# Attention stage of a two-layer trunk: own PSUM banks for the stick scores, head 0's scores inside the last projection slot, and the first output slot begun pair by pair

## Chip, cores and metric

One core of one Trainium2 chip. The metric is device time in microseconds, from start to end of one execution. The kernel is one program; nothing else runs on the core.

## What is computed

A trunk of two layers over 512 frames of width 1024. Layer 0 mixes by pooling and a state space; layer 1, where the change lies, mixes by two attentions, each of 8 heads of width 64. Every layer ends in a squared-ReLU MLP of width 4096. Cut to what the change touches:

```python
def _cd_mixer(h, w_in, w_out):
    qc, kc, vc, qi, ki, wi, qd, kd, vd = jnp.split(h @ w_in, offs, axis=-1)
    oc = _dsa_mixer(...)            # indexer picks 128 keys a query; softmax with ALiBi over them
    od = _stick_breaking_mixer(...) # z = q k^T / 8; log_keep = log_sigmoid(-z);
                                    # w = exp(log_sigmoid(z) + later sum of log_keep); w @ v
    return jnp.concatenate([oc, od], axis=-1) @ w_out
```

## The kernel before

**Engines and tiles.** Time lies in 4 blocks of 128 (NB = 4). Each of the engines has its own instruction stream, ordered by hand, with semaphores between them. TensorE (PE) has 8 PSUM banks of 512 float32. A weight slot is 1024 x 256: SyncE loads it, ScalarE (ACT) writes the rounded part `w_hi` (L707), VectorE (DVE) the rest `w_lo` (L1157), and PE makes 2 tiles of it, each of 8 products over k with 3 matmuls each (`product`): 48 matmuls a slot. Projection tiles go round banks 0 to 3. Slots of the values (`vd`, `vc`) are cut into 4 tiles, one for each block b.

**Projection of layer 1.** Slots in the order qi, ki, qd, kd, vd, qc, kc, vc, two slots each save ki. ACT copies every tile out (`copy_tile`, L765). From slot qd0 (`index_first`) on, PE also makes the indexer's scores, 8 a slot for three slots, ACT does their ReLU and DVE adds them to `score`. DVE then takes the 128 largest of blocks 1 to 3 in 48 rounds (MAX8 L1400 and MATCH_REPLACE8 L1402), 6 rounds a slot from the fourth of these slots on, and after the last slot writes `dsel` (`selected_distances`), the distances of the chosen keys.

**Attention steps.** Step s begins softmax head s and stick head s^1 and carries on those of the steps before. PE in step s: `scores(s,0)`, `scores(s,1)`, `outputs(s-2)`, `scores(s,2)`, `scores(s,3)`, `prob_transposes(s-1)`, `stick_sums(s-1)`. `scores(s,n)` is a pair of 64-row matmuls, which run beside each other: softmax scores into bank 4 + n%2, stick scores into bank n%2. Transposes go to bank 4 + n%2, the sums of the stick head (products of `sp_sb` with `tri` and `ones`) to bank 2 + j%2, outputs to banks 7 and 6. Because transposes share banks with the softmax scores, `prob_transposes(s-1)` waits until DVE has read rows n = 2 and 3 of step s (`s_used`).

DVE in step s: for n = 0 to 3 score plus ALiBi (L1454) and negated maximum (L1458), with `softplus_sum(s-1)` (L1441, 128 x 1280) after n = 1; then |z| into `sp_sb` (L1464); in steps 3, 5, 7 `out_lo` (L1436); then z minus the sums (L1473), four times; then four times a reciprocal (L1478) and a scaling (L1480). ACT in step s: z out of PSUM (L899), transposes out of PSUM (`pT`, L907), in steps 3, 5, 7 `out_hi` (L886), exponentials of the softmax (L916) and of the stick head (L923), then Exp and Ln of |z| (L926, L928). GpSimd (POOL) zeroes the non-causal part of four diagonal blocks (`keep_causal`, L650), of `sp_sb` after L1441 and of z after L923; PE's sums wait for the first, `outputs` for the second. Step 8 has no new scores, and step 9 only `outputs(7)`. After it ACT and DVE make the last pair of `h_hi` and `h_lo` tiles, and the four output slots (`plain_slots`) follow, then norm and MLP, in which PE is busy throughout.

## Time and profile before

| what | value |
|---|---|
| median of 3 runs | 1387.94 us (1386.94 to 1389.24) |
| the profiled execution | 1387.05 us, of which 1385.3 us span |
| PE, DVE, ACT, POOL busy | 91%, 59%, 32%, 12% of the span |
| last projection tile to first output matmul | 845.2 to 966.03 us |

The profiled execution is 0.9 us under the median. A timeline row gives the start in us from the start of the span, the duration, the engine, the line, the operation and its operands; "x4" merges neighbours of one kind, and brackets give the idle time of the engine before it and who ended it. PEclk is the share of full clock that TensorE was granted. Step s begins here where DVE starts L1454 of that step: step 6 at 923.7 and step 7 at 937.1 us.

### The profile page before, as it was taken

What the parts mean: (1) busy time and instruction counts of PE and PEld (TensorE: products, weight loads), DVE (VectorE), ACT (ScalarE), POOL (GpSimd) and SP (SyncE); (2) the same over time, 40 slices, a digit from 0 to 9 for tenths busy, and PEclk for the clock granted to TensorE, in tenths of its full rate; (3) what the DMA queues carried; (4) which work ended last, traced back from release to release, by engine and by line L of the source; (5) the groups of instructions that cost most, each with busy time, mean ns of one, the idle gap of its engine ahead of it and who ended that gap; (6) DMA issues with size and microseconds to landing.
All of it is one profiled execution on the core that took longest, in us unless ns stands there. A gap on an engine that the chain in (4) does not pass through costs nothing.

```text
span 1385.3 us, 16190 instructions
## 1 busy us (share of the span) xinstructions
PE 1265.3 (91%) x6140; PEld 1025.2 (74%) x6140; DVE 812.4 (59%) x1132; ACT 438.4 (32%) x589; POOL 159.8 (12%) x172
## 2 busy tenths in 40 slices
PE   4548858899999999999999997888999999999999
PEld 4347756688888888888877986555878888888887
DVE  2989887666555465556436797875363344343432
ACT  1223213133132141232334225775233132231321
POOL 1700540310000000006000000111400000000022
PEclk9769958999999999999999999999999999999999
DMA  8235745735444544453122331000323322323311
GB/s 261 68 99 148 195 128 187 238 114 188 162 157 164 168 159 165 151 185 91 61 92 62 97 110 37 1 1 1 91 84 99 91 91 91 91 91 105 103 64 61
DMA packets 136912, 157.68 MB, mean 114 GB/s; under 512 B 24168, under 2 KB 117536, under 8 KB 136864
## 3 DMA queue, kind: packets, MB, share of 16 engines
q1 hardware_dynamic: 121808, 151.72, 33.7%
q10 hardware_dynamic: 14480, 3.74, 1.5%
q0 software_dynamic: 576, 1.57, 0.4%
q8 instruction: 30, 0.49, 0.1%
q14 instruction: 18, 0.15, 0.0%
HBM read 151.65 MB, written 4.19 MB: 112 GB/s over the span
## 4 chain that ended last, share of the span: by engine, by line
PE 75%; DVE 16%; DMA 3%; ACT 2%; ACTq 2%; issue 1%; POOL 0%; DVEq 0%; SPq 0%
PE psum L1510 73%; DMA ada_ring<-in_ada_w 3%; DVE w_lo L1157 2%; DVE ada_acc L990 1%; PE psum L1514 1%; DVE work L1174 1%; ACTq L693 1%; DVE bz L961 1%; DVE h_lo L1186 1%; DVE sp_sb L1441 1%; DVE work L961 1%; ACT w_hi L707 1%; DVE s_t L961 1%; DVE work L1454 0%; DMA u_scratch<-ub 0%
## 5 line engine op out<-in xcount | busy, mean ns | idle before, releaser
L1510 PE MATMUL psum<-h_hi,w_hi 128*128 128x512 f32 x880 | 346.3, 394 | 18.0 <-DVE w_lo L1157 9.0
L1510 PE MATMUL psum<-h_lo,w_hi 128*128 128x512 f32 x880 | 343.8, 391 | 0.0
L1510 PE MATMUL psum<-h_hi,w_lo 128*128 128x512 f32 x880 | 343.5, 390 | 0.0
L707 ACT ACTIVATE w_hi<-w_raw 128x2048 fp32r<-128x2048 f32 x92 | 174.8, 1900 | 353.2 <-PE psum L1510 316.0
L1157 DVE TENSOR_TENSOR w_lo<-w_raw,w_hi 128x2048 fp32r<-128x2048 f32 x92 | 213.8, 2324 | 107.1 <-ACT w_hi L707 106.8
L1510 PEld LDWEIGHTS psum<-h_hi,w_hi 128*128 128x128 f32 x880 | 165.1, 188 | 58.7 <-issue 13.1
L1510 PE MATMUL psum<-a_hi,w_hi 128*128 128x512 f32 x512 | 202.4, 395 | 0.0
L1510 PE MATMUL psum<-a_hi,w_lo 128*128 128x512 f32 x512 | 202.2, 395 | 0.0
L1510 PE MATMUL psum<-a_lo,w_hi 128*128 128x512 f32 x512 | 202.1, 395 | 0.0
L1510 PEld LDWEIGHTS psum<-h_hi,w_lo 128*128 128x128 f32 x880 | 165.1, 188 | 35.7
L1510 PEld LDWEIGHTS psum<-h_lo,w_hi 128*128 128x128 f32 x880 | 165.3, 188 | 34.7
L1305 DVE SCALAR_TENSOR_TENSOR xT<-psum,mods,xT 128x512 f32<-128x512 f32 x80 | 59.2, 749 | 192.8 <-PE psum L1510 192.7
L1350 DVE TENSOR_TENSOR work<-work 128x512 f32<-128x512 f32 x64 | 44.2, 690 | 127.4 <-ACT work L840 126.6
L1510 PEld LDWEIGHTS psum<-a_hi,w_lo 128*128 128x128 f32 x512 | 96.3, 188 | 22.9
L1510 PEld LDWEIGHTS psum<-a_lo,w_hi 128*128 128x128 f32 x512 | 96.3, 188 | 22.8
L1510 PEld LDWEIGHTS psum<-a_hi,w_hi 128*128 128x128 f32 x512 | 96.3, 188 | 22.7
L840 ACT ACTIVATE work<-psum 128x512 f32<-128x512 f32 x64 | 38.2, 598 | 212.3 <-PE psum L1510 212.3
L562 POOL TENSOR_TENSOR sumsq<-xT 128x512 f32<-128x512 f32 x4 | 4.2, 1042 | 724.4 <-DVE xT L1305 724.4
L1340 DVE SCALAR_TENSOR_TENSOR ada_acc<-ada_l_ring,pb,ada_acc 128x768 f32<-128x768 f32 x56 | 60.0, 1071 | 1.1
L1354 DVE TENSOR_TENSOR a_lo<-work,a_hi 128x512 fp32r<-128x512 f32 x64 | 44.3, 692 | 2.6
L990 DVE SCALAR_TENSOR_TENSOR ada_acc<-ada_ring,pb,ada_acc 128x768 f32<-128x768 f32 x28 | 32.2, 1150 | 20.0 <-DMA ada_ring<-in_ada_w 18.5
L566 POOL TENSOR_TENSOR sumsq<-sumsq,work 128x512 f32<-128x512 f32 x24 | 43.7, 1819 | 1.9
(279 smaller groups left out, 1487.6 us busy)
## 6 DMA issues: line engine op xcount, KB each, us to landing
w_raw<-in_mlp_w SPq DMA_DIRECT2D x64, 1024.0 KB, 5.4
ada_l_ring<-in_ada_w SPq DMA_DIRECT2D x64, 384.0 KB, 6.1
ada_ring<-in_ada_w SPq DMA_DIRECT2D x40, 384.0 KB, 4.4
w_raw<-in_cd_w_in SPq DMA_DIRECT2D x14, 1024.0 KB, 5.1
ada_first<-in_ada_w SPq DMA_DIRECT2D x24, 384.0 KB, 3.9
w_raw<-in_ab_w_in SPq DMA_DIRECT2D x4, 1024.0 KB, 6.5
w_raw<-in_ab_w_out SPq DMA_DIRECT2D x4, 1024.0 KB, 8.2
w_raw<-in_cd_w_out SPq DMA_DIRECT2D x4, 1024.0 KB, 5.1
```

The source lines that it names most:

```text
L566: ins = pool.tensor_tensor(sumsq[:, :], sumsq[:, :], work[3][:, 0:L], ALU.add)
L693: act.dma_start(bb[ri][:, :, :], src[0].rearrange("(t g) p c -> (g p) t c", g=2)).then_inc(b_in, 16)
L707: act.activation(w_hi[n % 2][:, :, 0:w], raw[n % 2][:, :, 0:w], ACT.Copy).then_inc(hi_ready, 1)
L840: act.activation(work[t % 2][:, 0:L], bank[(t0 + t) % 4], ACT.Relu)\
L961: own(dve.tensor_tensor(o, a, b, op))
L990: ins = dve.scalar_tensor_tensor(out=acc[:, :], in0=buf[:, at_, :], scalar=pb[:, k:k + 1], in1=acc[:, :], op0=ALU.mult, op1=ALU.add)
L1157: dve.tensor_tensor(w_lo[n % 2][:, :, 0:w], raw[n % 2][:, :, 0:w], w_hi[n % 2][:, :, 0:w].bitcast(F32), SB).then_inc(lo_ready, 1)
L1305: dve.scalar_tensor_tensor(out=xT[:, k, :], in0=bank[t % 4], scalar=mods[:, a, 16 + k:17 + k], in1=xT[:, k, :], op0=M, op1=A).then_inc(dve ...
L1340: ins = dve.scalar_tensor_tensor(out=ada_acc[:, :], in0=src, scalar=pb[:, k:k + 1], in1=ada_acc[:, :], op0=M, op1=A)
L1350: dve.tensor_tensor(work[2][:, 0:L], work[t % 2][:, 0:L], work[t % 2][:, 0:L], M)\
L1354: dve.tensor_tensor(a_lo[:, t, :], work[2][:, 0:L], a_hi[:, t, :].bitcast(F32), SB)\
L1510: return nc.tensor.matmul(o, lhsT, rhs, start=start, stop=stop, **kw)
```

## The change

- PE: the stick scores go to banks 2 and 3 (6 and 7 for head 0), transposes and sums both to banks 0 and 1. So a transpose no longer waits for `s_used` of the next step but for `r_used` of the sums one step earlier, and the sums of j = 0, 1 now wait for `t_copied` of n = 2, 3. `scores` waits for `s_used` and `z_copied` alone.
- Head 0: PE issues `scores(0,0)`, `scores(0,1)` behind tile 0 and `scores(0,2)`, `scores(0,3)` behind tile 1 of the last slot (vc1). ACT takes the z copies, the exponentials and the table load into this slot, DVE `score_rows(0)` and `score_norms(0)`. In step 1 the transposes stand before `scores(1,2)`.
- DVE: selection starts with slot qd0, 3 rounds a slot for three slots, then 6; `dsel` is written as soon as the rounds are over. |z| is a bitwise AND with one SBUF source in place of an operation with two. The four reciprocals are one of 128 x 4, which waits for all four exponentials.
- PE: the first output slot's products (48 matmuls) go in four parts of 12, for k = (0,4), (1,5), (2,6), (3,7): behind `outputs(6)`, behind `stick_sums(7)`, behind `outputs(7)`, and after the last pair is ready. The three other slots follow.

```diff
--- before.py
+++ after.py
@@ -213,6 +213,9 @@
+    def score_bank(step, n):
+        return bank[(6 if step == 0 else 2) + n % 2]
...
@@ scalar engine @@
+        def z_copies(step, blocks):
+            z = z_sb[step % 3]
+            if step >= 3:
+                act.wait_ge(o_ps, step - 2)
+            for j in blocks:
+                act.wait_ge(z_ps, NB * step + j + 1)
+                act.activation(z[:, z_at[j]:z_at[j] + (NB - j) * P], score_bank(step, j)[:, 0:(NB - j) * P],
+                               ACT.Copy).then_inc(z_copied, 1)
+        def prob_exps(step, order):
+            for n in order:
+                i = NB - 1 - n
+                act.wait_ge(max_ready, NB * step + n + 1)
+                act.activation(probs(step, i), probs(step, i), ACT.Exp, bias=small[:, i:i + 1],
+                               accum_out=small[:, 8 + i:9 + i]).then_inc(p_exp, 1)
+        def soft_logs(step):
+            s_ = sp_sb[step % 2]
+            act.wait_ge(z_abs, step + 1)
+            own(act.activation(s_[:, :], s_[:, :], ACT.Exp, scale=-1.0))
+            settle()
+            act.activation(s_[:, :], s_[:, :], ACT.Ln, bias=eps_t[:, 1:2]).then_inc(z_soft, 1)
         for j, (name, half) in enumerate(cd_slots):
             n = CD_IN + j
             prep(n + 1)
             t0 = first_tile[n]
+            if n == CD_OUT - 1:
+                act.preload_act_table_set("natural_log_exp_and_others")
             if name == "ki":
                 copy_tile(t0, ki_t[:, :])
                 copy_tile(t0 + 1, wi_row[:, :], bank[(t0 + 1) % 4][0:8, :], scale=IDX_SCALE)
                 for b in range(NB):
                     copy_tile(t0 + b, qk[name][:, b, half * SLOT:(half + 1) * SLOT],
                               bank[(t0 + b) % 4][:, 0:SLOT])
+                    if n == CD_OUT - 1:
+                        if b < 2:
+                            z_copies(0, range(2 * b, 2 * b + 2))
+                        else:
+                            prob_exps(0, range(2 * b - 4, 2 * b - 2))
             else:
                 dst = qi_t if name == "qi" else qk[name]
                 for r in range(2):
...
-        act.wait_ge(tile_done, first_tile[CD_OUT])
-        act.preload_act_table_set("natural_log_exp_and_others")
...
+        soft_logs(0)
+        for step in range(1, H + 1):
             if step < H:
+                z_copies(step, range(2 if step == 1 else NB))
+            for n in range(NB):
+                i = NB - 1 - n
+                act.wait_ge(t_ps, NB * (step - 1) + n + 1)
+                if n == 0 and step >= 2:
+                    act.wait_ge(oc_ps, step - 1)
+                act.activation(pT[:, 0:i + 1, i * P:(i + 1) * P],
+                               bank[n % 2][:, 0:(i + 1) * P].rearrange("p (j q) -> p j q", q=P),
+                               ACT.Copy).then_inc(t_copied, 1)
+            if step == 1:
+                z_copies(step, range(2, NB))
             if step >= 3 and step % 2 == 1:
                 out_hi((step - 3) // 2)
             if step < H:
+                prob_exps(step, range(NB))
+            z = z_sb[(step - 1) % 3]
+            for j in range(NB):
+                act.wait_ge(r_used, NB * (step - 1) + j + 1)
+                v_ = z[:, z_at[j]:z_at[j] + (NB - j) * P]
+                act.activation(v_, v_, ACT.Exp).then_inc(w_exp, 1)
+            if step < H:
+                soft_logs(step)
@@ vector engine @@
+        def score_rows(step):
...
+            dve.wait_ge(z_copied, NB * (step + 1))
+            dve.tensor_scalar(sp_sb[step % 2][:, :].bitcast(I32), z_sb[step % 3][:, :].bitcast(I32),
+                              0x7fffffff, None, ALU.bitwise_and)\
+               .then_inc(z_abs, 1)
+        def score_norms(step):
+            dve.wait_ge(p_exp, NB * (step + 1))
+            own(dve.reciprocal(small[:, 12:12 + NB], small[:, 8:8 + NB]))
+            settle()
+            for n in range(NB):
+                i = NB - 1 - n
+                dve.tensor_scalar(probs(step, i), probs(step, i), small[:, 12 + i:13 + i], None, M)\
+                   .then_inc(p_ready, 1)
-            if n >= index_first + 3:
-                for _ in range(6):
+            if n >= index_first:
+                for _ in range(6 if n >= index_first + 3 else 3):
                     if rounds:
                         take_round(rounds.pop(0)[0])
...
-                dve.wait_ge(z_copied, NB * (step + 1))
-                dve.scalar_tensor_tensor(out=s_[:, :], in0=z[:, :], scalar=-1.0, in1=z[:, :],
-                                         op0=M, op1=ALU.max).then_inc(z_abs, 1)
...
-                    dve.wait_ge(p_exp, NB * step + n + 1)
-                    own(dve.reciprocal(small[:, 12 + i:13 + i], small[:, 8 + i:9 + i]))
...
@@ tensor engine @@
+        def scores(step, n):
+            i, j = NB - 1 - n, n
+            if step or n >= 2:
+                pe.wait_ge(s_used, NB * step + n - 1)
+            if step >= 2 or n >= 2:
+                pe.wait_ge(z_copied, NB * step + n - 1)
+            hs = stick_head(step)
+            p0, p1, t = HD * (step % 2), HD * (hs % 2), step // 2
+            mm(bank[4 + n % 2][:, 0:(i + 1) * P], qc[p0:p0 + HD, t, i * P:(i + 1) * P],
+               kc[p0:p0 + HD, t, 0:(i + 1) * P], True, True).then_inc(s_ps, 1)
+            mm(score_bank(step, n)[:, 0:(NB - j) * P], kd[p1:p1 + HD, t, j * P:(j + 1) * P],
+               qd[p1:p1 + HD, t, j * P:], True, True).then_inc(z_ps, 1)
+        def prob_transposes(pr):
+            for n in range(NB):
+                i = NB - 1 - n
+                pe.wait_ge(p_ready, NB * pr + n + 1)
+                if n >= 2:
+                    pe.wait_ge(t_copied, NB * pr + n - 1)
+                elif pr:
+                    pe.wait_ge(r_used, NB * (pr - 1) + n + 3)
+                for j in range(i + 1):
+                    last = transpose(bank[n % 2][:, j * P:(j + 1) * P], probs(pr, i)[:, j * P:(j + 1) * P])
+                last.then_inc(t_ps, 1)
+        def stick_sums(pr):
+            s_ = sp_sb[pr % 2]
+            pe.wait_ge(sp_ready, NB * (pr + 1))
+            for j in range(NB):
+                if j < 2:
+                    pe.wait_ge(t_copied, NB * pr + j + 3)
+                else:
+                    pe.wait_ge(r_used, NB * pr + j - 1)
+                o = bank[j % 2]
...
+                    if n == CD_OUT - 1 and b < 2:
+                        scores(0, 2 * b)
+                        scores(0, 2 * b + 1)
...
+        def first_out(ks):
+            t = first_tile[CD_OUT]
+            if ks[0] == 0:
+                slot_ready(CD_OUT)
+                pe.wait_ge(z_copied, NB * H)
+                for r in range(2):
+                    tile_free(t + r)
+            pe.wait_ge(cat_ready, 8 + 2 * (ks[0] + 1))
+            for k in ks:
+                for r in range(2):
+                    last = product(bank[(t + r) % 4], weight(CD_OUT, k, r * P), h(k), k == 0, k == 7)
+                    if k == 7:
+                        last.then_inc(tile_done, 1)
+        for step in range(1, H + 2):
             if step < H:
                 scores(step, 0)
                 scores(step, 1)
-            if step >= 2:
+            if step == 1:
+                prob_transposes(0)
+            else:
                 outputs(step - 2)
             if step < H:
                 scores(step, 2)
                 scores(step, 3)
-            if 1 <= step <= H:
+            if step == H:
+                first_out((0, 4))
+            if step == H + 1:
+                first_out((2, 6))
+            if 1 < step <= H:
                 prob_transposes(step - 1)
+            if step <= H:
                 stick_sums(step - 1)
+            if step == H:
+                first_out((1, 5))
         pe.wait_ge(cat_ready, 16)
-        plain_slots(CD_OUT, 4, cat_ready, 8)
+        first_out((3, 7))
+        for n in range(CD_OUT + 1, CD_OUT + 4):
+            slot_ready(n)
+            for r in range(2):
+                tile(n, first_tile[n] + r, r)
...
```

## Rows read from the trace of the kernel before

**Rows 1.** Profile page, busy us of each engine over the span

```profile
PE 1265.3 (91%) x6140; PEld 1025.2 (74%) x6140; DVE 812.4 (59%) x1132; ACT 438.4 (32%) x589; POOL 159.8 (12%) x172
```

**Rows 2.** Window of step 6: PE, PEld, DVE, ACT, POOL busy, PEclk, DMA share, GB/s

```profile
923.70:937.10 13.40, 11.36 (x66) 6.81 (x62) 10.17 (x23) 9.53 (x23) 2.44 (x8) 1.00 0.00 1
```

**Rows 3.** Timeline of all engines, step 6 into step 7

```profile
926.10 1.48 DVE L1441 SCALAR_TENSOR_TENSOR sp_sb<-z_sb,sp_sb 128x1280 f32<-128x1280 f32 x1
...
927.65 1.03 POOL L650 TENSOR_SCALAR_AFFINE_SELECT sp_sb<-sp_sb 128x128 f32<-128x128 f32 x4 [4.89 <-DVE sp_sb L1441]
...
928.05 1.17 PE L1514 MATMUL psum<-ident,probs_b 128*128 128x128 f32 x7 [1.76 <-DVE work L1454]
...
928.80 1.48 DVE L1464 SCALAR_TENSOR_TENSOR sp_sb<-z_sb 128x1280 f32<-128x1280 f32 x1
...
929.91 0.60 ACT L907 ACTIVATE pT<-psum 128x256 f32<-128x256 f32 x2 [0.16 <-PE psum L1514]
...
930.03 1.08 PE L1510 MATMUL psum<-sp_sb,tri 128*128 128x512 f32 x2
...
934.78 0.69 PE L1510 MATMUL psum<-kc,qc 64*128 64x512 f32 x1
...
934.93 1.24 POOL L650 TENSOR_SCALAR_AFFINE_SELECT z_sb<-z_sb 128x128 f32<-128x128 f32 x3 [0.77 <-ACT z_sb L923]
...
935.28 0.49 DVE L1480 TENSOR_SCALAR work<-work,small 128x512 f32<-128x512 f32 x1
...
936.48 0.64 PE L1510 MATMUL psum<-pT,vc 128*64 128x512 f32 x1
...
936.71 1.36 ACT L928 ACTIVATE sp_sb<-sp_sb,eps_t 128x1280 f32<-128x1280 f32 x1
...
937.14 0.68 DVE L1454 SCALAR_TENSOR_TENSOR probs_b<-dsel,psum 128x512 f32<-128x512 f32 x1
...
939.44 0.27 PE L1510 MATMUL psum<-qd,kd 64*128 64x128 f32 x1
```

**Rows 4.** Selection: VectorE on `score` (min/median/max ns), and its timeline in slot qd1

```profile
L1400 DVE MAX8 small<-score x48: 421/561/696, 750.7 to 834.9; 128x8 f32<-128x256 f32 x16, 128x8 f32<-128x384 f32 x16, 128x8 f32<-128x512 f32 x16
...
718.52 2.29 DVE L1157 TENSOR_TENSOR w_lo<-w_raw,w_hi 128x2048 fp32r<-128x2048 f32 x1 [1.02 <-ACT w_hi L707]
```

**Rows 5.** Timelines of VectorE, ScalarE and PE from the last slot to step 1

```profile
836.47 2.29 DVE L1157 TENSOR_TENSOR w_lo<-w_raw,w_hi 128x2048 fp32r<-128x2048 f32 x1
...
845.25 0.38 ACT L765 ACTIVATE vc<-psum 128x256 f32<-128x256 f32 x1 [2.49 <-PE psum L1510]
845.66 1.28 ACT L889 ACT_TABLE_LOAD   x1
...
850.82 0.50 ACT L916 ACTIVATE work<-work,small 128x256 f32<-128x256 f32 x1
...
855.33 0.45 PE L1510 MATMUL psum<-kc,qc 64*128 64x256 f32 x1 [3.87 <-ACT z_sb L899]
...
860.87 1.92 PE L1510 MATMUL psum<-sp_sb,tri 128*128 128x512 f32 x2
```

**Rows 6.** Busy time and granted clock in step 1; columns as in rows 2

```profile
856.50:862.80 6.30, 4.44 (x13) 2.82 (x14) 3.88 (x6) 3.26 (x10) 1.03 (x4) 0.50 0.00 0
```

**Rows 7.** Timeline of all engines, steps 7 to 9 and first output slot

```profile
943.93 1.61 PE L1510 MATMUL psum<-sp_sb,tri 128*128 128x512 f32 x2
...
955.17 1.97 PE L1510 MATMUL psum<-sp_sb,tri 128*128 128x512 f32 x2 [1.37 <-POOL sp_sb L650]
...
961.66 0.64 PE L1510 MATMUL psum<-pT,vc 128*64 128x512 f32 x1
...
966.03 0.50 PE L1510 MATMUL psum<-h_hi,w_hi 128*128 128x512 f32 x1 [2.00 <-DVE h_lo L1436]
...
966.98 2.29 DVE L1157 TENSOR_TENSOR w_lo<-w_raw,w_hi 128x2048 fp32r<-128x2048 f32 x1 [1.00 <-ACT w_hi L707]
...
976.57 0.75 DVE L1305 SCALAR_TENSOR_TENSOR xT<-psum,mods,xT 128x512 f32<-128x512 f32 x1 [7.30 <-PE psum L1510]
```

More of the change, by code:

```diff
@@ L859, in index_relu, with out_hi @@
                                ACT.Relu).then_inc(idx_rel, 1)
+        def out_hi(pair):
+            for tile, b, signal in ((pair, 7, oc_ps), (4 + pair, 6, o_ps)):
+                act.wait_ge(signal, 2 * pair + 2)
+                act.activation(h_hi[:, tile, :], bank[b], ACT.Copy).then_inc(cat_hi, 1)
+        def z_copies(step, blocks):
[18 more added lines that the diff above has]
+            act.activation(s_[:, :], s_[:, :], ACT.Ln, bias=eps_t[:, 1:2]).then_inc(z_soft, 1)
         for j, (name, half) in enumerate(cd_slots):
@@ L1419, in selected_distances @@
             dve.sem_inc(dsel_ready, 1)
-        for j, (name, half) in enumerate(cd_slots):
-            n = CD_IN + j
-            prep(n + 1)
-            for r in range(2):
-                index_scores(index_group(n, r))
-            if n >= index_first + 3:
-                for _ in range(6):
-                    if rounds:
-                        take_round(rounds.pop(0)[0])
-        assert not rounds
-        selected_distances()
         def out_lo(pair):
@@ L1442, in softplus_sum @@
                                      in1=sp_sb[head % 2][:, :], op0=ALU.max, op1=A).then_inc(sp_diag, 1)
-        for step in range(H + 1):
+        def score_rows(step):
+            for n in range(NB):
+                i = NB - 1 - n
+                w = (i + 1) * P
+                dve.wait_ge(s_ps, NB * step + n + 1)
+                if step >= 2:
+                    dve.wait_ge(t_ps, NB * (step - 2) + n + 1)
+                dve.scalar_tensor_tensor(out=probs(step, i), in0=dsel[:, sel_at[i]:sel_at[i] + w],
+                                         scalar=-SLOPES[step], in1=bank[4 + n % 2][:, 0:w],
+                                         op0=M, op1=A).then_inc(s_used, 1)
+                dve.wait_ge(s_used, NB * step + n + 1)
+                dve.reduce_max(small[:, i:i + 1], probs(step, i), AX_X, negate=True)\
+                   .then_inc(max_ready, 1)
+                if n == 1 and step >= 1:
+                    softplus_sum(step - 1)
+            dve.wait_ge(z_copied, NB * (step + 1))
[10 more added lines that the diff above has]
+                   .then_inc(p_ready, 1)
+        for j, (name, half) in enumerate(cd_slots):
+            n = CD_IN + j
+            prep(n + 1)
+            for r in range(2):
+                index_scores(index_group(n, r))
+            if n >= index_first:
+                for _ in range(6 if n >= index_first + 3 else 3):
+                    if rounds:
+                        take_round(rounds.pop(0)[0])
+                        if not rounds:
+                            selected_distances()
+            if n == CD_OUT - 1:
+                assert not rounds
+                score_rows(0)
+                score_norms(0)
+        for step in range(1, H + 1):
             if step == H:
@@ L1447, in _ @@
             if step < H:
-                for n in range(NB):
-                    i = NB - 1 - n
-                    w = (i + 1) * P
-                    dve.wait_ge(s_ps, NB * step + n + 1)
-                    if step >= 2:
-                        dve.wait_ge(t_ps, NB * (step - 2) + n + 1)
-                    dve.scalar_tensor_tensor(out=probs(step, i), in0=dsel[:, sel_at[i]:sel_at[i] + w],
-                                             scalar=-SLOPES[step], in1=bank[4 + n % 2][:, 0:w],
-                                             op0=M, op1=A).then_inc(s_used, 1)
-                    dve.wait_ge(s_used, NB * step + n + 1)
-                    dve.reduce_max(small[:, i:i + 1], probs(step, i), AX_X, negate=True)\
-                       .then_inc(max_ready, 1)
-                    if n == 1 and step >= 1:
-                        softplus_sum(step - 1)
@@ L1482, in _ @@
+            if step < H:
+                score_norms(step)
         out_lo(H // 2 - 1)
```

130 lines of the change are left out of this document (36 added, 94 removed).

## Prediction

> **What bounds the kernel now.** I read the page first: PE is busy 91% of the span [rows 1], so a gain must come from a stretch where PE waits or from work moved into such a stretch. Outside the attention steps of layer 1 PE is nearly solid around the change; inside them it is not. The window of step 6 [rows 2] shows 13.4 us with PE busy 11.36, DVE 10.17, ACT 9.53: no engine is full, so a chain through several engines sets the period. The timeline of that step [rows 3] shows it. PE's transposes start at 928.05 after 1.76 us idle, and the row names DVE's L1454, that is the wait for `s_used` of rows n = 2, 3, which stand behind the 1.48 us `softplus_sum` on DVE. The sums follow at 930.03, though POOL had `sp_sb` ready at 927.65 + 1.03 = 928.7. So the shared bank delays the sums by 1.3 us, everything behind them (z minus sums, norms, next scores) by as much, and PE idles about 2 us a step.
>
> **The change, the steps.** I count the new period from the start T of a head's sums.
>
> PE's loop, all from [rows 3]: sums 930.03 to 934.78, 4.75; two score pairs to 936.48, 1.70; outputs and the last two score pairs to 939.71, 3.23; then transposes without the old wait. They must be copied before the sums may start, since both now use banks 0 and 1: from 928.05 to the third copy (half of the 0.60 at 929.91), 2.2. Together 11.9; the ends of pipelined matmuls overlap the next start by about 0.1, so 11.8.
>
> DVE's and POOL's loop: from T the norms begin 5.06 later (0.19 ahead of the scaling at 935.28), and took 2.05 until 937.14. One reciprocal in place of four takes away three times about 0.19: 1.48, T + 6.5. From L1454 to `softplus_sum` are 926.10 - 923.74 = 2.36, from there to POOL 1.55, POOL 1.03 and 0.05 of handover: T + 11.55. PE's loop is the longer, by 0.25. ACT has Ln done at 938.07, T + 8.0, and DVE wants it at T + 8.9. The new waits: the norms wait for all four exponentials, which ACT issues before the stick exponentials and so before T + 5; `scores(s,2)` waits for the first z copy, due T + 8.5 against T + 8.75 on PE. In steps 3 and 5, `out_hi` and `out_lo` (1.1 and 1.3 us) fall between T and T + 2.4, where DVE would idle.
>
> |z| with one source: 1.48 now; its nearest row is the scaling, 0.49 for 512 columns, so at most 1.2 for 1280 and about 0.8 if half of that is fixed. I take no gain for it: DVE has it done before T + 1, and the first subtraction is due at T + 2.4. With that cover gone it would be worth 0.3 to 0.7 a step. The Trainium skill (SBUF — State Buffer, section on the two separate sides) states that a DVE operation in a two-port mode and a GpSimd operation lock each other out for the whole instruction, which speaks against this edit; the trace agrees as far as it goes, since POOL's three blocks beside the scaling took 1.24 and four blocks without it 1.03 [rows 3]. By that rule the sum would lose something only if |z| met POOL's `sp_sb` blocks; it starts 2.7 us after `softplus_sum` started, and POOL ends 2.6 after, so the sum is the same by the rule with about 0 to 0.8 a step of risk.
>
> From the sums of head 0 to those of head 6 are six periods. Before: 943.93 - 860.87 = 83.1 [rows 5, 7]. After: 6 x 11.8 = 70.8. **Gain 12.3.** Bounds: 11.55 a step (POOL's loop) gives 13.8; 12.6 a step (below) gives 7.5.
>
> **The change, the head.** Selection: the same 48 rounds on DVE, nine of them in three earlier slots, 3 a slot. A round of width 256 is MAX8 0.42 [rows 4], MATCH_REPLACE8 about as long and a load of 0.1: 2.9 us for three, against 1.02 us of idle before `w_lo` in such a slot [rows 4]. So `w_lo` comes about 1.9 late; `w_lo` of the next slot is made while PE works at this one, and at 836.47 it was done 6.4 before the slot's end at 845.2 [rows 5], which hides it. If that cover were gone it would be 1.9 a slot, 5.7 at most. In return the rounds end with slot kc1, `dsel` is ready there, and DVE is free when vc1 begins.
>
> In vc1 the four score pairs stand between tiles: 1.70 for two, and 0.8 for the last two (the 3.23 above less 2.4 for outputs, below), 2.5 on PE's path. They wait for copies of z and for L1454, which follows `w_lo` at 838.8 [rows 5]; the third pair is wanted at 841.2. The table load, 1.28 [rows 5], moves before the first tile copy; no tile waits for that bank, so nothing. The last tile was copied at 845.25 [rows 5]; now 847.7, ready 848.1. Behind it ACT has two exponentials of 0.5 or less (850.82 is one) with their reads, 1.0; norms 1.5; 2.36 to `softplus_sum`; 1.55 to POOL; 1.08: sums of head 0 at 848.1 + 7.5 = 855.6. Before: 860.87. **Gain 5.3.** What was late before (PE idle 3.87 before 855.33, then the transposes behind L1454) is gone; now the softmax chain of head 0 is.
>
> The clock: in step 1 PE was granted 0.50, 1.2 GHz, in a stretch of 6.3 us behind the idle of 3.87 [rows 5, 6]; two 128x512 sums took 1.92 instead of 1.08 [rows 3, 5]. Now PE will idle about 3 us before the third transpose, as ACT does Exp and Ln of head 0 first. I take a fall as likely and charge **1.1** (sums of head 0 slower by some 1.1 before DVE can go on; bounds 0 and half of the 4.44 busy there, 2.2). The Trainium skill (TensorE: Matmul & The Clock Gate, What's actually happening) states that full rate is what activity releases and idleness takes away; the rows agree. By it fuller steps hold 2.4 GHz, and step 6 with 2 us idle held it anyway [rows 2].
>
> **The change, the tail**, from the start T of head 6's sums. Now: 943.93 to the end of the first output slot, where DVE takes its tile at 976.57, PE free at 976.4: 32.5 [rows 7]. After: sums 4.75; `outputs(6)` 2.4 (961.66 to 964.03, the idle of 2.00 before 966.03 taken off); 12 output matmuls. A slot of 48 took 976.4 - 966.03 = 10.4, so 2.6. Transposes and copies 2.2; T + 11.95. `sp_sb` of head 7 is ready at about T + 10.7, so of the 2.6 only 1.4 were hidden. Sums 4.75; second part 2.6, not hidden (`outputs(7)` could start at once, as now at 961.66); `outputs(7)` 2.4; third part 2.6, which hides the 2.0 of `h_hi` and `h_lo`; fourth part 2.6: T + 26.9. The next slot's `w_lo` ends 5.24 after `outputs(7)` (969.27 - 964.03), T + 26.95. So T + 27.0. **Gain 5.5**, of which 3.4 is hidden work and the rest the slow-clock sums at 955.17 (1.97) and 943.93 (1.61) that PE no longer makes cold. Bounds: 3.4 less if nothing is hidden; 1 more if `w_lo` is no limit.
>
> **Sum.** 12.3 + 5.3 - 1.1 + 5.5 = 22.0. On the profiled execution 1387.05 - 22.0 = 1365.05; the median of the three runs lies 0.9 higher: **1366**. Everything behind is PE-bound and moves with it; the weights of the next slots are loaded long before.
>
> **Rivals.**
> - *Handovers take the place of the wait.* Three waits that were covered become PE's own: for the z copy, for the copy ahead of the third transpose, for the third copy ahead of the sums. At 0.2 to 0.3 each (DVE, ACT and PE follow each other at such distances in rows 3) a step is 12.6, six cost 4.8 more, 1371. For it: ACT meets PE within 0.25. Against: POOL's loop has the same length and would not add.
> - *Steps fully packed.* PE's handovers overlap and no clock falls: 11.55 a step, 1.5 less, and 1.1 less: 1363. Against: a PE loop of 11.8 in the rows.
> - *The tail doesn't do what it says.* The parts stand in front of transposes and `outputs(7)` in PE's order, and hide nothing: 3.4 lost, with `w_lo` late by up to 2: 1371.
> - *Slower: half clock.* With PE waiting in new places (step 1, third transpose) the clock stays at 1.2 GHz in the steps. Then 11.36 us of PE work take 22.7, 10.9 more than 11.8 a step. Two such steps eat the gain, from the third on it is slower; four give 1366 + 44 = 1410. For it: the stretch at 0.50. Against: the clock came back there under load, and step 6 held 1.00 with more idleness than the new steps have.
>
> **How the numbers follow.** Forecast (1363.5 to 1369) 0.60; handovers 0.19; packed 0.11; tail 0.05; half clock 0.05, of which 0.02 with two such steps (within 0.2%) and 0.03 with more. 0.2% is 2.8 us, about what a measurement of this kernel tells from no change. Faster 0.95, same 0.02, slower 0.03. The range takes in packed and handovers with their spread: 1360 to 1374.
>
> **What would show it.** Right: L1454 of the even and odd steps 11.6 to 12.1 us apart in steps 2 to 7; transposes directly behind the scores, with no wait for DVE; sums starting within 0.3 of both POOL's end and the third copy; PEclk 1.00 in the steps but perhaps step 1; sums of head 0 near 855.6; first output matmuls inside step 8 and slot 2 about 27 us behind head 6's sums. Wrong: L1454 12.5 or more apart (handovers or DVE); PE idle before `w_lo` of the slots kd0 to vd0 (selection moved too early); POOL's blocks over 0.4 each beside L1464's successor; PEclk 0.50 in several steps.

## The result, and the profile after

| what | before | after |
|---|---|---|
| median, run side by side | 1388.59 us (1386.94 to 1390.21) | 1365.99 us (1365.35 to 1367.21) |
| ratio, 95% interval | | 0.9838 (0.9821 to 0.9855) |
| the profiled execution | 1387.05, span 1385.3 | 1367.21, span 1365.5 |
| sums of head 0, of head 6, second output slot begins | 860.87, 943.93, 977.05 | 857.22, 930.44, 958.12 |

The forecast was 1366.0 in a range of 1360 to 1374. The change is faster by 22.6 us between the medians, and by 19.8 between the two profiled executions. In the profiled one of after everything lies 1.34 later already before the change begins (`wi_row` is copied at 702.78 instead of 701.44), which is an uncertainty of such comparisons and none of the change's.

The page of after, busy us and share of the span (as [rows 1]): all engines do about the same work in 20 us less.

```profile
PE 1264.2 (93%) x6140; PEld 1026.9 (75%) x6140; DVE 804.4 (59%) x1108; ACT 437.7 (32%) x589; POOL 158.8 (12%) x172
```

Two windows of after, from the sums of heads 3 and 4 to the next head's; columns as in [rows 2]. PE is busy 11.29 us in a step, about as before (11.36), but the step is 12.03 long, not 13.40.

```profile
894.34:906.37 12.03, 11.29 (x62) 6.84 (x63) 9.12 (x20) 9.45 (x24) 2.34 (x8) 1.00 0.00 0
906.37:918.41 12.04, 11.29 (x63) 6.85 (x63) 10.43 (x22) 10.42 (x26) 2.58 (x8) 1.00 0.01 1
```

The timeline of after in the second of these windows, to be laid beside [rows 3]. L1540 are the transposes, L930 their copies, L1446 `softplus_sum`, L1465 |z|, L876 the copies of z.

```profile
906.37 1.10 PE L1536 MATMUL psum<-sp_sb,tri 128*128 128x512 f32 x2 [0.30 <-ACT pT L930]
...
911.45 0.17 DVE L1471 RECIPROCAL small<-small 128x4 f32<-128x4 f32 x1
...
915.27 1.48 DVE L1446 SCALAR_TENSOR_TENSOR sp_sb<-z_sb,sp_sb 128x1280 f32<-128x1280 f32 x1
...
916.00 0.99 PE L1540 MATMUL psum<-ident,probs_b 128*128 128x128 f32 x7
...
916.82 1.03 POOL L653 TENSOR_SCALAR_AFFINE_SELECT sp_sb<-sp_sb 128x128 f32<-128x128 f32 x4 [4.17 <-DVE sp_sb L1446]
...
917.43 0.68 PE L1540 MATMUL psum<-ident,probs_b 128*128 128x128 f32 x3 [0.45 <-ACT pT L930]
...
917.88 0.55 ACT L930 ACTIVATE pT<-psum 128x256 f32<-128x256 f32 x2 [0.21 <-PE psum L1540]
917.97 0.82 DVE L1465 TENSOR_SCALAR sp_sb<-z_sb 128x1280 int32<-128x1280 int32 x1
...
918.41 1.10 PE L1536 MATMUL psum<-sp_sb,tri 128*128 128x512 f32 x2 [0.30 <-ACT pT L930]
```

The transposes at 916.00 follow the scores with no wait for DVE; in [rows 3] they had one of 1.76 there. PE now has two short waits, both for ACT's copies: 0.45 before the third transpose and 0.30 before the sums. Only the second is new. A wait before the third transpose stood in the kernel before as well, and from the first transpose to the third PE took 1.41 then and 1.43 now:

```profile
929.46 0.73 PE L1514 MATMUL psum<-ident,probs_b 128*128 128x128 f32 x3 [0.24 <-ACT pT L907]
```

The waits of after from 870 to 930 (us in total, times, longest), five steps, say the same; beside the issue of weight loads, these are the largest of PE.

```profile
PEld psum L1536 <- POOL sp_sb L653: 2.3, 5, 0.5
PE psum L1540 <- ACT pT L930: 2.3, 5, 0.5
PE psum L1536 <- ACT pT L930: 1.5, 5, 0.3
```

The chain that ended last (start, us, what) stays with PE and ACT from the sums of head 0 on, and from 942.71 on with PE alone; DVE, whose row n = 2 ended the wait in [rows 3], is not in it there.

```profile
857.22 10.71 PE psum L1536 x52
867.93 0.60 PE psum L1540 x4
868.55 0.61 ACT pT L930
...
870.27 9.69 PE psum L1536 x52
...
942.71 48.25 PE psum L1536 x216
```

### The profile page after: what moved, and what is told of

It reads as the page before. It is cut to its first block, busy times and chain, and to the rows that moved or that the text cites. A ratio compares the mean times of both kernels' runs of the same rounds, so it can differ in the third digit from the quotient of the medians.

```text
span 1365.5 us, 16163 instructions
## 1 busy us (share of the span) xinstructions
PE 1264.2 (93%) x6140; PEld 1026.9 (75%) x6140; DVE 804.4 (59%) x1108; ACT 437.7 (32%) x589; POOL 158.8 (12%) x172
## 4 chain that ended last, share of the span: by engine, by line
PE 78%; DVE 13%; DMA 4%; ACT 2%; ACTq 2%; issue 1%; POOL 0%; DVEq 0%; SPq 0%
PE psum L1536 77%; DMA ada_ring<-in_ada_w 3%; DVE ada_acc L1007 2%; DVE w_lo L1174 1%; DVE work L1191 1%; ACTq L696 1%; DVE bz L978 1%; PE psum L1540 1%; DVE h_lo L1203 1%; DVE work L978 1%; ACT w_hi L710 1%; ACT pT L930 1%; DVE s_t L978 1%; DMA u_scratch<-ub 1%; DVE bd L1148 0%
```

## The experiments

The ratios are to the kernel before, run beside each group. "Period" is the distance between the sums of two heads that follow each other, in the profiled execution; the kernel before has 13.4, 13.4, 13.9, 13.9, 14.0 and, for the first, 14.5, the change 12.03, and 13.05 for the first.

**1. The change once more**, to see what two profiled executions have in common.

> The changed kernel once more, as the base for the others of this group. All theories: ratio to the kernel before 0.982 to 0.986; sums of neighbouring heads 12.0 us apart, sums of head 0 about 13 before those of head 1.

Measured: 1366.12 (1362.88 to 1370.76), ratio 0.9843 (0.9815 to 0.9871). Periods 2 to 6 are 12.03 again. The first is 14.78, and the windows of this execution in step 1 show the granted clock at 0.50:

```profile
858.00:862.00 4.00, 3.89 (x6) 2.15 (x7) 1.24 (x4) 2.07 (x8) 0.05 (x1) 0.50 0.02 4
862.00:866.00 4.00, 4.00 (x17) 2.88 (x18) 1.94 (x5) 1.46 (x3) 0.53 (x2) 0.80 0.00 0
```

So the first period varies between executions of one kernel; in these two the others do not. I call such a stretch at half clock a fall. I compare periods 2 to 6 from here on, and the first by itself.

**2. Banks alone**: the kernel before with the new bank assignment and its waits, nothing else.

```diff
-            if step >= 2 and n < 2:
-                pe.wait_ge(t_copied, NB * (step - 2) + n + 3)
-            elif step or n >= 2:
+            if step or n >= 2:
...
-                if pr + 1 < H and n < 2:
-                    pe.wait_ge(s_used, NB * (pr + 1) + n + 3)
-                else:
+                if n >= 2:
...
+                elif pr:
+                    pe.wait_ge(r_used, NB * (pr - 1) + n + 3)
```

> The kernel before with the bank assignment and its waits alone (stick scores in banks 2 and 3, transposes and sums in 0 and 1). Theory (the wait for the next step's rows made the step): steps go from 13.4 to about 12.1 us (DVE's and GpSimd's loop with four reciprocals 11.55 + 0.57), the six from head 0 to head 6 from 83 to about 73, 9 to 10 us gain in all. Rival (VectorE's shorter work made the step): steps stay at 13 or more, gain below 3.

Measured: 1378.24, ratio 0.994 (0.992 to 0.996), 9.0 us. Periods 12.16. The forecast's loop over DVE and POOL, 11.55 with one reciprocal, is 12.12 with four. And POOL is what the sums now wait for (waits of PE, 876 to 935):

```profile
PE psum L1510 <- POOL sp_sb L650: 2.0, 5, 0.4
PE psum L1514 <- ACT pT L907: 1.8, 4, 0.5
```

**3. The four reciprocals back** in the changed kernel:

```diff
-            dve.wait_ge(p_exp, NB * (step + 1))
-            own(dve.reciprocal(small[:, 12:12 + NB], small[:, 8:8 + NB]))
-            settle()
             for n in range(NB):
                 i = NB - 1 - n
+                dve.wait_ge(p_exp, NB * step + n + 1)
+                own(dve.reciprocal(small[:, 12 + i:13 + i], small[:, 8 + i:9 + i]))
+                settle()
```

> The changed kernel with four reciprocals in place of one. Theory (TensorE's loop 12.03 bounds, VectorE's and GpSimd's was 0.5 under it and becomes 12.1): period 12.1 to 12.2, 1 us slower in all. Rival (VectorE's loop is the bound, each of its operations counts in full): 12.6, 4 us slower.

Measured: 1366.06 (1364.64 to 1367.64), ratio 0.9849 (0.9833 to 0.9866). Periods 12.16, as in experiment 2, and again PE waits for POOL before the sums (1.6 us in 4 waits, 870 to 928). So with the new banks the three reciprocals saved are worth 0.13 a step, not 0.57: beyond that PE's loop is the longer. The time itself can't tell 0.8 us.

**4. The two DVE edits alone**, in the kernel before: one reciprocal, |z| as an AND.

```diff
-                dve.scalar_tensor_tensor(out=s_[:, :], in0=z[:, :], scalar=-1.0, in1=z[:, :],
-                                         op0=M, op1=ALU.max).then_inc(z_abs, 1)
+                dve.tensor_scalar(s_[:, :].bitcast(I32), z[:, :].bitcast(I32),
+                                   0x7fffffff, None, ALU.bitwise_and).then_inc(z_abs, 1)
...
+                dve.wait_ge(p_exp, NB * (step + 1))
+                own(dve.reciprocal(small[:, 12:12 + NB], small[:, 8:8 + NB]))
+                settle()
```

> The kernel before, with two DVE edits of the change alone: one reciprocal of 128 x 4 in place of four, and |z| as a bitwise AND with one source; banks, head, selection and tail as before. Theory A (in the kernel before the period is the chain norms, L1454, transposes, sums, in which DVE's norms stand): each step is shorter by the three reciprocals saved, 0.5 to 0.6 us, that is 13.3 instead of 13.85 on average, 3 to 4 us in all (ratio about 0.997); |z| gives nothing, since its reader is due later. Rival B (the norms are hidden in the kernel before too, behind ACT's or PE's part): below 0.2 us a step and below 1 us in all. Rival C (|z| is on the path before the change, since the subtractions stand behind it): up to 0.7 us a step more than A, some 8 us in all.

Measured: 1383.58, ratio 0.9969 (0.9955 to 0.9984): 4.7 us by the medians. Periods 12.91 to 12.93. Against the 13.4 periods of before that is 0.49, theory A (the norms, from the first reciprocal to the next L1454, took 1.56 instead of 2.05). But three of the five steady periods of before are 13.9 to 14.0, and there the difference is about 1.0. Theory A doesn't explain that half, nor does rival C, since in [rows 3] |z| ends before the sums can be subtracted. The windows of the kernel before do. The transposes stand behind the same idle of 1.76 in each step; in step 3 (886.0) and step 7 (940.0) the clock fell behind it, in steps 2, 4, 5 and 6 it didn't. The windows show step 3 and step 4. The fall in step 3 lengthens two periods, since it slows the transposes ahead of the sums at 889.24 and those sums themselves.

```profile
886.00:890.20 4.20, 3.26 (x12) 2.01 (x13) 2.96 (x6) 2.13 (x6) 1.03 (x4) 0.63 0.00 0
899.00:903.20 4.20, 2.16 (x18) 1.35 (x15) 4.13 (x7) 1.69 (x5) 1.03 (x4) 1.00 0.00 2
```

```profile
886.81 2.64 PE L1514 MATMUL psum<-ident,work 128*128 128x128 f32 x10 [1.76 <-DVE probs_b L1454]
...
901.24 1.17 PE L1514 MATMUL psum<-ident,probs_b 128*128 128x128 f32 x7 [1.76 <-DVE work L1454]
```

With the DVE edits the idle is 1.26 and no steady step shows a fall. One execution of each is profiled, so that the shorter idle prevents the fall is likely and not shown.

**5. |z| with two sources back** in the changed kernel.

```diff
-            dve.tensor_scalar(sp_sb[step % 2][:, :].bitcast(I32), z_sb[step % 3][:, :].bitcast(I32),
-                              0x7fffffff, None, ALU.bitwise_and)\
+            dve.scalar_tensor_tensor(out=sp_sb[step % 2][:, :], in0=z_sb[step % 3][:, :], scalar=-1.0,
+                                     in1=z_sb[step % 3][:, :], op0=M, op1=ALU.max)\
```

> The changed kernel with |z| made as before, by a DVE operation with two sources (1.48 us instead of 0.82). Theory A (|z| is hidden: DVE has it done before the first sums are to be subtracted): the period stays 12.03 and the time that of the changed kernel within 1.5 us. Rival B (|z| is on DVE's path in the changed kernel): the period grows by up to 0.66, to 12.7, and the time by 4 to 5 us.

Measured: 1366.62 (1365.46 to 1370.15), ratio 0.9849 (0.983 to 0.9868), periods 12.03. The edit takes 0.66 us a step off DVE (1.48 to 0.82) and nothing off the time that the runs can tell.

**6. The first output slot back behind the heads.**

```diff
-            if step == H:
-                first_out((0, 4))
-            if step == H + 1:
-                first_out((2, 6))
...
-            if step == H:
-                first_out((1, 5))
...
-        first_out((3, 7))
...
+        plain_slots(CD_OUT, 4, cat_ready, 8)
```

> The changed kernel with the first output slot back behind all heads; nothing else differs. Theory (hidden work): from the sums of head 6, sums 4.75, outputs 2.4, transposes and copies 2.35, wait for GpSimd until 10.7, sums 4.75, outputs 2.4, conversion of the last pair 2.1, slot 10.4: 30.4 us where the changed kernel took 27.7, so 2.7 slower, and up to 1.7 more if TensorE falls to half clock in the sums of head 7 as it did before the change. Rival (parts stand in the way): the parts in front of the transposes and of outputs(7) give back what they hide, within 0.7 us of the changed kernel.

Measured: 1372.83, ratio 0.9902 (0.9884 to 0.992), 6.7 above the change by the medians; its profiled execution has no clock fall in step 1. From the sums of head 6 to the second output slot it has 32.5 (928.44 to 960.93) where the change has 27.7: **4.8**, above the 4.4 that I allowed. It is made, within 0.1, of the 2.7 expected, of 1.6 of half clock, and of 0.6 because I took the slot at 10.4 where it is 11.0 (the same misreading as in the prediction, see the tail below). The other 1.9 between the medians is not accounted for. The timeline of PE shows the idle times that the pieces of output had filled (1.37 and 2.00), and behind the second of them eight distances between output products of 0.43 instead of 0.23, that is the 1.6 us. I had allowed for a fall in the sums of head 7; they ran at full clock, and it came in the slot.

```profile
939.17 1.13 PE L1536 MATMUL psum<-sp_sb,tri 128*128 128x512 f32 x2 [1.37 <-POOL sp_sb L653]
...
948.34 0.50 PE L1536 MATMUL psum<-h_hi,w_hi 128*128 128x512 f32 x1 [2.00 <-DVE h_lo L1441]
...
950.61 0.63 PE L1536 MATMUL psum<-h_hi,w_hi 128*128 128x512 f32 x1
951.04 0.63 PE L1536 MATMUL psum<-h_lo,w_hi 128*128 128x512 f32 x1
...
955.27 0.39 PE L1536 MATMUL psum<-h_hi,w_lo 128*128 128x512 f32 x1
955.50 0.39 PE L1536 MATMUL psum<-h_hi,w_hi 128*128 128x512 f32 x1
```

**7. Head 0 back behind the last slot.**

```diff
-                    if n == CD_OUT - 1 and b < 2:
-                        scores(0, 2 * b)
-                        scores(0, 2 * b + 1)
...
+        for n in range(NB):
+            scores(0, n)
```

(and its z copies and exponentials on ACT behind the last tile copy)

> The changed kernel with head 0's scores, z copies, exponentials, rows and norms behind the last projection slot; nothing else differs. Theory: the softmax chain of head 0 then starts at the end of the slot; sums of head 0 about 2.4 us later than in the changed kernel, 1 more if the clock falls longer: 2.4 to 3.5 slower. Rival (the 2.5 us of scores that now lengthen the slot cancel it): within 0.7.

Measured: 1370.68, ratio 0.9881 (0.986 to 0.9901). From the copy of `wi_row` to the sums of head 0 it has 156.79, the change 154.44: 2.35, as expected. The medians differ by 4.6. The first period is 14.9 in its profiled execution, but 14.78 in that of experiment 1, so a fall doesn't explain the other 2.2; where they come from is open.

**8. The gap of step 1 filled** with ten products of the identity with itself, into an unused bank, between the second and the third transpose.

```diff
-                prob_transposes(0)
+                prob_transposes(0, (0, 1))
+                for _ in range(10):
+                    mm(bank[7][:, 0:P], ident[:, :], ident[:, :], True, True)
+                prob_transposes(0, (2, 3))
```

> The changed kernel with ten 128x128 products of the identity (thrown away, into bank 7) between the second and third transpose of head 0 in step 1, where TensorE idles 2.2 us. Theory (the granted clock, not the work, makes the first period 12.05, 13.05 or 14.8 us in different executions): sums of head 0 to head 1 in 12.0 to 12.2, PEclk 1.00 from 850 to 870, time 1 to 2.5 us under the changed kernel's and with less spread. Rival (the first period is long because ScalarE does Exp and Ln of head 0 first): it stays at 13 or more, whatever the clock.

Measured: 1364.18 (1363.92 to 1369.31), ratio 0.9846 (0.9825 to 0.9868). The first period is 12.06, the granted clock 1.00 throughout. The first window is of this kernel, the second of the change, each around the start of the sums of head 0:

```profile
854.00:858.00 4.00, 3.23 (x12) 2.15 (x13) 2.47 (x6) 2.53 (x11) 0.72 (x3) 1.00 0.01 4
```

```profile
856.00:858.00 2.00, 1.52 (x7) 0.87 (x6) 1.65 (x6) 1.57 (x5) 1.03 (x4) 0.50 0.00 0
```

So a fall costs 1.0 in the profiled change and 2.7 in experiment 1. The added work costs nothing: the sums of head 0 come 154.44 after `wi_row`, in both. This fits the Trainium skill (TensorE: Matmul & The Clock Gate, What's actually happening), by which the full rate hangs on how busy PE has been.

That the filling is what kept the clock up is not shown by this run alone. The same idle of 2.18, unfilled, stood in step 1 of experiments 3, 6 and 9, with no fall (first periods 12.16, 12.05 and 11.84), while it fell in the change, in experiments 1 and 5, and behind 2.28 in experiment 7. So unfilled it fell in four profiled executions of seven, and filled in none of four (experiments 8, 10, 11 and 12), which speaks for the filling and isn't proof. Experiment 9's gap and the window around it, unfilled and at full clock:

```profile
855.12 0.68 PE L1542 MATMUL psum<-ident,work 128*128 128x128 f32 x3 [2.18 <-ACT pT L932]
```

```profile
852.00:860.00 8.00, 4.96 (x29) 3.39 (x28) 6.37 (x14) 6.60 (x18) 1.03 (x4) 1.00 0.00 0
```

The time doesn't show a gain either: the ratio is no lower than the change's 0.9838 and 0.9843, and the spread that was expected to shrink is 5.4 us.

**9. Another order on PE**: `scores(s,3)` (in step 8 the first output part) between the second and the third transpose.

```diff
+            if 1 < step <= H:
+                prob_transposes(step - 1, (0, 1))
+            if step < H:
                 scores(step, 3)
...
-                prob_transposes(step - 1)
+                prob_transposes(step - 1, (2, 3))
```

(on ACT the fourth z copy moves ahead of the third transpose copy)

> The changed kernel with scores(s,3), or the first part of the output slot in step 8, between the transposes of n = 1 and n = 2, and the fourth z copy before the third transpose copy. Theory (TensorE's own loop of 12.03 is the bound, with 0.45 and 0.29 us of waits for ScalarE's copies in it, and GpSimd's loop lies 0.5 under it): period 11.6 to 11.7, and 2 to 3 us gain. Rival (VectorE and GpSimd already bound the step): 12.0, no gain.

Measured: 1364.81 (1362.75 to 1366.9), ratio 0.9837 (0.982 to 0.9854). Periods 11.81 (the first 11.84), and 11.59 for head 7, against 12.03 and 12.27. The wait of 0.45 is gone and the one of 0.30 stayed; weight loads wait for POOL as in the change (1.8 us in 4 waits, 870 to 926, against 2.3 in 5). The period was expected at 11.6 to 11.7. The ratio is the change's, so the gain of 2 to 3 us that was expected isn't seen in the time.

**10. The same, with the gap filled and `softplus_sum` behind row n = 0** in place of n = 1.

```diff
-                if n == 1 and step >= 1:
+                if n == 0 and step >= 1:
```

> The two edits before together, and softplus_sum on VectorE one row earlier (behind n = 0). Theory: GpSimd's blocks are ready 1 us earlier, TensorE's loop without the first copy wait remains: period 11.3 to 11.5, sums of head 0 up to 1 earlier, the clock holds in step 1: 5 to 7 us under the changed kernel, 1360. Rival (row n = 1 now stands behind softplus_sum and holds scores(s,3)): period 11.7 or more, gain under 4.

Measured: 1362.33 (1360.16 to 1363.74), ratio 0.9816 (0.9799 to 0.9832). Periods 11.81 still: I had expected 11.3 to 11.5, and that step of the reasoning fell. The time is 3.7 under the change by the medians, where I expected 5 to 7. These are the rival's numbers, but not its mechanism: PE doesn't wait for row n = 1, and experiment 12 has the same row behind `softplus_sum` with a period of 11.32. The weight loads' wait for POOL is gone; only the 0.30 for ACT is left.

**11. All four transpose copies ahead of the last z copy** on ACT.

```diff
-                if n == 2 and 1 < step < H:
-                    z_copies(step, range(3, NB))
...
             if step < H:
+                z_copies(step, range(2 if step == 1 else 3, NB))
```

> The version with the reordered steps, the warm first step and softplus_sum behind n = 0, in which ACT now takes the last z copy behind all four transpose copies instead of ahead of the third. Theory A (in that version the third transpose copy, queued behind the last z copy, gates the sums by 0.29 us a step): the period falls from 11.81 to 11.5 to 11.6, 1.5 to 2 us less in all. Theory B (the period is held by DVE and POOL, through softplus_sum and keep_causal): the period stays 11.8 and the sums then wait for sp_sb from POOL. Theory C (the later z copy makes |z| late, and the z minus sums operations with it): over 11.9.

Measured: 1362.97 (1361.28 to 1364.56), ratio 0.9824 (0.9805 to 0.9842), periods 11.81. Theory A is refuted: the last z copy no longer stands before the third transpose copy, and the wait is the same. Theory B isn't it either: the sums wait for ACT, and no wait of PE names POOL.

```profile
PE psum L1536 <- ACT pT L930: 1.5, 5, 0.3
```

```profile
912.38 0.68 PE L1540 MATMUL psum<-ident,probs_b 128*128 128x128 f32 x3
...
912.82 0.55 ACT L930 ACTIVATE pT<-psum 128x256 f32<-128x256 f32 x2 [0.21 <-PE psum L1540]
...
913.35 1.10 PE L1536 MATMUL psum<-sp_sb,tri 128*128 128x512 f32 x2 [0.30 <-ACT pT L930]
```

From the start of the last three transposes at 912.38 (two of n = 2, one of n = 3) to the sums are 0.97: 0.44 until ACT starts, 0.38 for the copy of 256 columns, 0.15 back to PE; the fourth transpose covers only part of it. It is a round trip that needs cover, whatever ACT's order is.

**12. The transposes interleaved with the scores**: transposes 0 and 1, `scores(s,2)`, transpose 2, `scores(s,3)`, transpose 3, sums (base: experiment 10).

```diff
+            if 1 < step <= H:
+                prob_transposes(step - 1, (0, 1))
             if step < H:
                 scores(step, 2)
             if 1 < step <= H:
-                prob_transposes(step - 1, (0, 1))
+                prob_transposes(step - 1, (2,))
             if step < H:
                 scores(step, 3)
...
-                prob_transposes(step - 1, (2, 3))
+                prob_transposes(step - 1, (3,))
```

(on ACT the third z copy ahead of the third transpose copy, the fourth ahead of the fourth)

> The version with the reordered steps, the warm first step and softplus_sum behind n = 0, with another order on PE in steps 2 to 7: transposes n = 0, 1, then scores(s,2), transpose n = 2, scores(s,3), transpose n = 3, sums; ACT takes the last two z copies ahead of the third and the fourth transpose copy. Theory A (the period of 11.81 is PE's own work, 11.5, plus one uncovered round trip of 0.3 from the third transposes over ACT's copy back to PE's sums): scores(s,3) now hides it, the sums follow their transposes without a wait for ACT, and the period is 11.5 to 11.55, about 1.7 us less in all than the versions at 11.81. Theory B (the period of 11.81 is held by DVE, through the second row of scores behind softplus_sum): scores(s,3) starts later than PE comes to it, and the period stays 11.7 to 11.9. Theory C (the copies on ACT come too late in this order): over 11.9.

Measured: **1360.68** (1359.12 to 1362.03), ratio 0.9802 (0.9785 to 0.982), the fastest of all, 5.3 under the change by the medians. Periods 11.32. The period was expected at 11.5 to 11.55. The 0.49 off 11.81 is the wait of 0.30 and 0.2 that I hadn't counted: the rows behind the outputs take PE 2.56 (909.65 to 912.21) where they took 2.74 without the wait (910.31 to 913.35, less 0.30). A window of it shows PE with no idle at all:

```profile
890.00:902.00 12.00, 12.00 (x65) 7.12 (x64) 9.81 (x21) 10.13 (x24) 2.57 (x8) 1.00 0.01 2
```

## Why the prediction held, step by step

**The mechanism of the steps was right, its size a little off.** The wait for DVE in front of the transposes left, and PE's loop became the longer, with the loop over DVE and POOL just behind: measured 11.48 for the latter (from the sums at 906.37 to POOL's end at 917.85), forecast 11.55, and experiments 2 and 3 show it ending last when three reciprocals come back. Of the signs named beforehand, the sums start 0.15 after the third copy, as said, but 0.56 after POOL's end, not within 0.3. The sums, the scores and the outputs took PE 9.63 together (906.37 to 916.00), forecast 9.68. The term that was mis-sized is the last one of PE's loop. I gave 2.2 from the first transpose to the sums, less 0.1 for overlap. It is 2.41 (916.00 to 918.41). I had read the end of the third copy as half of a row that merges two copies (0.60), but the copy of 256 columns is the longer one (0.38), and I left out the 0.15 from its end to PE's next start; in the kernel before the sums didn't wait for it. The 9.63 and the 2.41 make the 12.03; the 0.1 taken off for overlap wasn't there. Six periods gained 83.06 - 73.22 = 9.8, after the 1.0 that the clock took; forecast 12.3 - 1.1 = 11.2.

The rival *handovers* named three waits at 0.2 to 0.3 apiece. One of them came as new, the third copy ahead of the sums, and it costs the 0.23 a step. The one ahead of the third transpose was already in the rows that gave the 2.2 (0.24 at 929.46), and the one for the z copy never showed. The rival *packed* is excluded for this kernel; experiment 12 shows that what it asks for, and less than its 11.55, can be had by the order of PE, ACT and DVE alone.

**What the forecast didn't see in the kernel before**: two falls behind the 1.76 idle, in steps 3 and 7, made three of its five steady periods about half a microsecond longer (experiment 4). I had used 83.1 as measured, so the sum took this in without naming it. With the DVE edits alone and with the banks alone no steady step has one in the profiled execution, which is a likely reason, not tested by itself, why their gains alone (12.9 and 12.16 from a mean of 13.7, 0.8 and 1.6 a step) make more than both together (1.7).

**The head.** Sums of head 0 at 857.22, less the 1.34, are 855.9; forecast 855.6, and 5.0 gained instead of 5.3. The last slot grew by 2.9 (forecast 2.5). Experiment 7 prices the move of head 0 alone at 2.35 of the 5.0.

**Selection** was free as said: `w_lo` of slot qd1 starts at 721.82, against 718.52 [rows 4], 2.0 late after the 1.34 (forecast 1.9), and no slot moved up to the last. In the last slot DVE is free early and waits for ACT, where it came straight from the selection before (836.47, [rows 5]):

```profile
837.29 2.29 DVE L1174 TENSOR_TENSOR w_lo<-w_raw,w_hi 128x2048 fp32r<-128x2048 f32 x1 [8.13 <-ACT w_hi L710]
```

**The clock in step 1** was charged 1.1 and cost 1.0 in the profiled execution of the change (2.7 in experiment 1, nothing in others, see experiment 8); the gap before the third transpose was 2.18, forecast about 3.

```profile
854.83 0.68 PE L1540 MATMUL psum<-ident,work 128*128 128x128 f32 x3 [2.18 <-ACT pT L930]
...
857.22 2.08 PE L1536 MATMUL psum<-sp_sb,tri 128*128 128x512 f32 x2 [0.47 <-POOL sp_sb L653]
```

The rival *half clock* didn't come: the steady steps are granted 1.00.

**The tail.** Gain 5.4 (33.1 to 27.7), forecast 5.5 (32.5 to 27.0). Both ends were 0.6 to 0.7 too early for the same reason: I took the time at which DVE picks up the first tile (976.57) for the end of the slot, but in the first slot the two tiles are made side by side, and the second slot begins at 977.05. So a slot is 11.02 and a part of 12 products 2.75, not 2.6. All else is as forecast, down to `w_lo` just in time:

```profile
937.50 0.50 PE L1536 MATMUL psum<-h_hi,w_hi 128*128 128x512 f32 x1
...
942.71 1.10 PE L1536 MATMUL psum<-sp_sb,tri 128*128 128x512 f32 x2 [0.29 <-ACT pT L930]
...
955.57 2.29 DVE L1174 TENSOR_TENSOR w_lo<-w_raw,w_hi 128x2048 fp32r<-128x2048 f32 x1 [1.00 <-ACT w_hi L710]
...
958.12 0.39 PE L1536 MATMUL psum<-h_hi,w_hi 128*128 128x512 f32 x1
```

Part of this gain is clock, as the forecast named it: the kernel before made the sums at 943.93 and 955.17 cold. Its output products behind the 2.00 idle ran 0.23 apart, so a slow slot is no part of the 5.4; in experiment 6 the same idle was followed by one, which makes 1.6 of its 4.8.

**|z|** and POOL: no cost and no gain, as said (experiment 5). POOL's blocks of `sp_sb` take 294 ns each against 296 before, but this tests no exclusion between the two engines, since |z| never runs beside them: it starts at 917.97, and POOL ends at 917.85. Beside the scalings the traces do show one, before and after alike: the block of z that starts at 911.70, inside the scaling of 911.65 to 912.14, takes 0.59 instead of 0.29, and the one at 935.35 before took 0.57.

```profile
911.70 0.59 POOL L653 TENSOR_SCALAR_AFFINE_SELECT z_sb<-z_sb 128x128 f32<-128x128 f32 x1
```

This agrees with the lock that the Trainium skill states (SBUF — State Buffer, SBUF: two separate sides). But by the same sentence of it a DVE operation with two SBUF inputs shuts out a GpSimd operation that reads SBUF too. So the rule spoke against the old form of |z| as much as against the new one, which the prediction left out.

**The sum.**

| gain, us | forecast | measured in the profiled executions |
|---|---|---|
| head | 5.3 | 5.0 |
| steps, with the clock in step 1 | 12.3 - 1.1 = 11.2 | 9.8 |
| tail | 5.5 | 5.4 |
| around the next norm | none | 0.9, may be scatter |
| all | 22.0 | 21.1 |

The profiled executions differ by 19.8, being 1.34 apart beforehand. That the medians (22.6) hit the forecast so closely is luck by about 1 us: the steps were over-forecast by 1.4, against the 0.9 behind and the scatter.

## What to carry to other kernels

When a shared bank's wait is removed, look at the waits that were covered by it. Each is a round trip (here 0.44 until the copy starts, 0.38 for the copy, 0.15 back). Putting independent matmuls into it took it away (experiments 9 and 12); moving a copy on ACT did not (experiment 11). Loops within about half a microsecond of each other (here 12.03 and 11.48) make edits worth less together than alone, so price each against the next loop, not against the present one. And an idle of PE of about 2 us can cost as much again in clock behind it, by chance from one execution to the next. Ten thrown-away products in the gap cost nothing, and no execution that had them fell there; a gain in time from them was not measured.

## What the runs showed of the hardware

- The granted clock didn't follow from the length of an idle alone. Behind the same 1.76 us it fell in steps 3 and 7 and not in steps 2, 4, 5 and 6 of the kernel before. Behind 2.18 in step 1 it fell in two executions of the change (first periods 13.05 and 14.78) and in experiment 5 (15.05), and not in experiments 3, 6 and 9 (12.16, 12.05, 11.84). It makes a difference of up to 3 us between executions of nearly the same code.
- After 2.00 us of idle, half clock can come a little later: in experiment 6 the first products run 0.34 and 0.23 apart, and only from the third on 0.43. Behind the same 2.00 the kernel before kept 0.23 (966.60, 966.84, 967.06).
- A bitwise AND of 128 x 1280 with one source took 0.82 us, the form with two sources 1.48; a reciprocal of 128 x 4 took 0.17, one of 128 x 1 0.16.
- GpSimd's 128 x 128 select took 0.29 us, and 0.57 to 0.59 where it began during a VectorE scaling between SBUF tiles (935.35 before, 911.70 after).
- From the start of the last three transposes over ScalarE's copy of 128 x 256 out of PSUM back to TensorE's next start were 0.97 us: 0.44, 0.38 and 0.15.
